# Start of a two-layer decoder trunk: held weight loads, first group's terms by readiness, matmuls over zeros

## What is computed

```python
for l in range(DEPTH):
    y = mixer_sublayer(x, w_in[l], lbs[l], a_norm_w[l], c_sinks[l], w_out[l], cos, sin)
    x = layer_norm(ALPHA * x + y, ln1_g[l], ln1_b[l])
    y = conv_ffn(x, w_gate[l], w_up[l], conv_w[l], conv_b[l], w_down[l])
    x = layer_norm(ALPHA * x + y, ln2_g[l], ln2_b[l])
```

## Time and profile before

| | us |
|---|---|
| median of 3 runs | 2239.49 |
| lowest, highest | 2239.21, 2239.70 |
| the profiled execution, its own time | 2238.69 |
| its span in the profile | 2236.9 |
| TensorE busy | 2207.1 (99%) |
| VectorE busy | 1391.9 (62%) |
| ScalarE busy | 1028.4 (46%) |
| GpSimd busy | 221.6 (10%) |

### The profile page before, as it was taken

How to read it: one execution, slowest core, us unless ns; L and a number is a source line. 1 busy time by engine, 2 the same in 40 slices (tenths; PEclk the granted TensorE clock), 3 DMA queues, 4 the chain that set the end, 5 groups by cost and what they waited for, 6 DMA issues and landing times.

```text
span 2236.9 us, 31431 instructions
## 1 busy us (share of the span) xinstructions
PE 2207.1 (99%) x11372; PEld 1889.1 (84%) x11372; DVE 1391.9 (62%) x1750; ACT 1028.4 (46%) x1286; POOL 221.6 (10%) x245
## 2 busy tenths in 40 slices
PE   8999999999999999999999999999999999999997
PEld 6888887888888888888888888888888888888886
DVE  5556666776666666545485566667766666664545
ACT  5444454544444444333454445554444444443332
POOL 1651000120000000000007310002100000000000
PEclk9999999999999999999999999999999999999999
DMA  8555465666666666666665555656666666666664
GB/s 294 171 163 170 144 221 156 202 189 185 191 188 188 187 188 205 221 194 193 185 193 169 160 160 152 226 164 193 185 191 191 189 182 194 188 226 198 193 193 132
DMA packets 214740, 420.25 MB, mean 188 GB/s; under 512 B 13024, under 2 KB 15104, under 8 KB 213632
## 3 DMA queue, kind: packets, MB, share of 16 engines
q1 hardware_dynamic: 212224, 406.90, 59.9%
q0 software_dynamic: 2432, 12.22, 1.5%
HBM read 416.97 MB, written 2.10 MB: 187 GB/s over the span
## 4 chain that ended last, share of the span: by engine, by line
PE 97%; DVE 1%; POOL 1%; ACT 0%; DMA 0%; issue 0%; DVEq 0%; POOLq 0%; ACTq 0%; SPq 0%
PE ps L1088 29%; PE ps L1044 17%; PE ps L1046 17%; PE ps L1045 17%; PE ps L1092 15%; PE ps L1182 1%; PE ps L1133 1%; PE ps L1156 0%; PE ps L1189 0%; PE ps L1202 0%; PE ps L1203 0%; PE ps L1201 0%; DMA raw<-in_w_in_dram 0%; DVE xres L803 0%; DVE xres L809 0%
## 5 line engine op out<-in xcount | busy, mean ns | idle before, releaser
L734 DVE TENSOR_TENSOR wlo<-raw,whi 128x1024 fp32r<-128x1024 f32 x768 | 952.2, 1246 | 757.2 <-ACT whi L524 753.9
L524 ACT ACTIVATE whi<-raw 128x1024 fp32r<-128x1024 f32 x768 | 807.1, 1058 | 966.5 <-PE ps L1046 460.7
L1088 PE MATMUL ps<-xT,whi 128*128 128x512 f32 x2816 | 657.2, 390 | 1.7 <-DVE xT L744 1.0
L1088 PEld LDWEIGHTS ps<-xT,whi 128*128 128x128 f32 x2816 | 522.4, 188 | 107.8 <-ACT qkT L539 2.1
L1044 PE MATMUL ps<-whi,xT 128*128 128x512 f32 x960 | 385.3, 401 | 9.9 <-DVE wlo L734 9.4
L1046 PE MATMUL ps<-whi,xT 128*128 128x512 f32 x960 | 375.2, 391 | 0.0
L1045 PE MATMUL ps<-wlo,xT 128*128 128x512 f32 x960 | 374.6, 390 | 0.0
L1092 PEld LDWEIGHTS ps<-xT,wlo 128*128 128x128 f32 x2816 | 350.0, 192 | 7.2
L1092 PE MATMUL ps<-xT,wlo 128*128 128x256 f32 x2816 | 352.2, 283 | 0.0
L1046 PE MATMUL ps<-whi,hT 128*128 128x512 f32 x704 | 273.9, 389 | 0.0
L1044 PE MATMUL ps<-whi,hT 128*128 128x512 f32 x704 | 273.9, 389 | 0.0
(11 more groups left out here) (158 smaller groups left out, 1070.5 us busy)
## 6 DMA issues: line engine op xcount, KB each, us to landing
raw<-in_w_in_dram SPq DMA_DIRECT2D x176, 512.0 KB, 3.9
raw<-in_w_gate_dram SPq DMA_DIRECT2D x176, 512.0 KB, 4.3
raw<-in_w_up_dram SPq DMA_DIRECT2D x176, 512.0 KB, 4.2
raw<-in_w_down_dram SPq DMA_DIRECT2D x176, 512.0 KB, 4.6
raw<-in_w_out_dram SPq DMA_DIRECT2D x64, 512.0 KB, 4.6
mix<-in_x_t_dram SPq DMA_DIRECT2D x8, 256.0 KB, 6.8
xres<-in_x_dram POOLq DMA_DIRECT2D x4, 512.0 KB, 8.4
lnb<-in_ln_g_dram POOLq DMA_DIRECT2D x2, 1024.0 KB, 7.8
```

The costliest lines, as they stand in the source:

```text
L524: act.activation(whi[:, s, :, :], raw[:, s, :, :], ACT.Copy).then_inc(hi_done, 1)
L734: dve.tensor_tensor(wlo[:, s, :, :], raw[:, s, :, :], whi[:, s, :, :].bitcast(F32), ALU.subtract)\
L1088: ins = pe.matmul(ps[:, bank, :], whi[:, s, kk, cols], xT[:, kt, :, :].rearrange("p a s -> p (a s)"), start=kt == 0, stop=kt == KT - 1)
```

## The change

Three edits, all at the start of layer 0:

- SyncE waits for the landing of weight group 0 before it issues x 1 (and with it weights 1), and for the landing of group 1 before it issues x 2 (and weights 2). All loads from x 3 on have no new wait.
- TensorE runs the first group by a new function, `first_group`. Its 12 matmuls are ordered by term: four of high weights with high x, which wait for `hi_done` and `xhi_done` only; four of low weights, which wait for `lo_done`; four with the low part of x, which wait for `x_ready`. The other groups are as before.
- VectorE first clears one half of `prob`, and TensorE runs three fp32 matmuls of 384 columns over these zeros into bank 7, whose content is overwritten later.

```diff
+                        if layer == 0 and i == 0 and 1 <= j <= 2:
+                            sp.wait_ge(raw_in[j - 1], 16)
                         if layer == 0 and i == 0:
                             sp.dma_start(mix[:, GK * j:GK * (j + 1), :], x_t[j * GK * P:(j + 1) * GK * P, :].rearrange(
...
+            dve.memset(prob[:, 0, :], 0.0).then_inc(warm_set, 1)
...
+            pe.wait_ge(warm_set, 1)
+            for n in range(3):
+                pe.matmul(ps[:, 7, 0:3 * P], prob[:, 0, 0:P], prob[:, 0, :], start=True, stop=True)
...
+            def first_group():
+
+                pe.wait_ge(hi_done, 1)
+                pe.wait_ge(xhi_done, 1)
+                terms = ((whi, 0), (wlo, 0), (whi, 1))
+                for n, (w, part) in enumerate(terms):
+                    if n == 1:
+                        pe.wait_ge(lo_done, 1 + CREDIT)
+                    if n == 2:
+                        pe.wait_ge(x_ready, 1)
+                    for t, kk in itertools.product(range(TT), range(GK)):
+                        ins = pe.matmul(ps[:, in_banks(0)[t], :], xT[:, kk, part, t * P:(t + 1) * P], w[:, 0, kk, :],
+                                        start=n == 0 and kk == 0, stop=False)
+                ins.then_inc(pe_used, 1)
...
-                        if i == 0:
+                        if i == 0 and layer + j > 0:
                             pe.wait_ge(x_ready, layer * 24 + (j + 1))
...
-                    rows_times_chunk(layer, p, xT, kts, banks, j == 0, j == GC - 1)
+                    if layer + p == 0:
+                        first_group()
+                    else:
+                        rows_times_chunk(layer, p, xT, kts, banks, j == 0, j == GC - 1)
```

More of the change, by code:

```diff
@@ L276, in program @@
         ln1_in, ln2_in = sem("ln1_in"), sem("ln2_in")
-        spare_set = sem("spare_set")
+        spare_set, warm_set = sem("spare_set"), sem("warm_set")
         lb_max, lb_exp = sem("lb_max"), sem("lb_exp")
```

## The result

The changed kernel takes 2244.15 us (median of 16 runs, 2242.22 to 2246.22), the kernel before 2239.32 (16 runs, 2238.33 to 2240.09). The ratio is 1.0021 with a 95% interval of 1.0014 to 1.0028, so the change costs 4.8 us. The spread of the runs more than doubled. The profiled execution of the changed kernel took 2242.95, 1.2 us under its median, and its span is 2241.2 against 2236.9.

The account below looks back on a forecast made before the run. TensorE's string of matmuls, 97% of the last chain, was taken to bound the kernel. Held loads start group 2 at 19.5 against 16.68 us, so 2239.5 + 2.8 = 2242.3 us, range 2239.0 to 2244.6.

Parts of the forecast that it names:

- First group by readiness: TensorE, group 0: first four matmuls wait for high parts alone, landing + 1.2 us instead of + 2.46, so 1.3 us earlier.
- The bound in the text: TensorE's opening wait: zeros even four times as dear would end by 9.2 us, and only then would they push group 0.
- group 0 would run at the low clock: TensorE, group 0: taken at 1.2 GHz, matmuls 0.43 us apart, ending at 12.3 us; said not to enter the sum.
- w0: Weight load of group 0: 4.3 us from issue with nothing behind it, landing at 5.9 us, 1.0 us earlier than before.
- w1 and w2: Weight loads of groups 1 and 2, held back: landing at 10.8 us (9.34 before) and 17.1 us (11.44 before).
- The burst: GpSimd's bias, level, flip, anorm and sinks loads, 0.66 MB, move forward 2 to 4 us and delay group 2's weights 0.4 us.
- w3 and the next land 2.1 us apart: Weight loads behind group 2's land faster than TensorE's 2.7 us per group, so nothing else stops TensorE in this stretch.
- what would prove me wrong: Signs against the forecast, among them TensorE idle ahead of group 3 or later, read as the burst hitting group 3's weights.
- The sum: TensorE: group 1 waits to 13.3 us, group 2 to 19.5 against 16.68, 2.8 us later, with nothing given back behind.
- The rival of the clock: TensorE's 3.5 us gap ahead of group 2 drops the clock, 1.81 us more: 4.6 us later, 2244.1 us, chance 0.16.
- The rival of the gain: All loads at the quick end, group 2's weights before 14.2 us: the hold pays, 2237.8 to 2239.5 us, chance 0.14.
- The rule on DMAs: Issue early, wait late speaks against the two waits; its page's figures give an estimated loss of 1 us.

Follow-up runs that it names:

- no_hold: The changed kernel without SyncE's two waits, zeros and new first group kept: 2237.39 us, ratio 0.9991 to the kernel before.
- hold_only: The kernel before with SyncE's two waits alone, no zeros and first group as before: 2242.29 us, ratio 1.0014.
- first_only: The kernel before with the new first group alone, no zeros and no held loads: 2238.28 us, ratio 0.9997.
- hold_zeros_8: The changed kernel, both waits kept, with eight matmuls over zeros instead of three: 2243.31 us.
- late_burst: The changed kernel with GpSimd's five small loads waiting for group 5 instead of group 0: 2240.48 us, ratio 1.0007 to the kernel before.
- hold_1: The changed kernel with only the first wait (x 1 and weights 1 wait for weights 0): 2239.7 us.
- hold_2: The changed kernel with only the second wait (x 2 and weights 2 wait for weights 1): 2240.05 us.

## Why the prediction was right, and where not

The forecast was 2242.3, slower, by the held loads, with 2239.0 to 2244.6 as the range. 2244.15 lies in it, near its upper end, and the direction and the cause were right: no_hold and hold_only show it. The size was not: 4.8 us slower against the 2.8 forecast.

- **First group by readiness.** Forecast: 1.3 us earlier against the kernel before, plus what the landing gains. The first matmul came 1.35 us earlier, of which 0.2 is the landing. first_only has it at 8.18, 1.2 earlier. Right.
```profile
73.03 1.78 PE ps L1145 x16
```

That makes 0.66 us for 384 columns at the high clock and 4.0 for three at the low one. They ended 1.7 us before the first high part was ready, so they cost nothing. The bound in the text was set against the wrong moment: zeros that end at 9.2 would not have pushed the old start at 9.39, but they would have pushed the new one at 7.1, as eight of them did in hold_zeros_8. That group 0 would run at the low clock was so in the profile for its first half (1.84 us for four matmuls; its last four start at 11.38 and take some 1.1).
- **w0.** Forecast 5.9, measured 6.73. The step "With x0 in front of it but nothing behind, I put w0 at 4.3 us" failed: 5.05 us from issue to landing with nothing behind, against 5.3 in company. Over all profiles it is 4.75 to 5.05 with x 1 held and 4.86 to 5.38 without. The gain that the holds should buy was 0.2 us and not 1.0.
- **w1 and w2.** Forecast 10.8 and 17.1, measured 11.14 and 15.53. From issue to landing both took 4.0 us. w1 came 0.3 us late, w0's 0.8 less what its own load was quicker. For w2 I took 5.3 us because loads would stand behind it, and this term was too large by 1.3. With the 0.4 for the burst, which hit nothing there, w2 came 1.6 us earlier than I said, and group 2 at 17.99 and not at 19.5.
- **The burst.** This is the step that failed most. I gave it 0.4 us, on w2. It hit w4, which took 9.9 us from issue (13.60) to landing (23.53), and cost 3.7 us by late_burst. The step from "w3 and the next land 2.1 us apart" to "nothing else stops TensorE in this stretch" was wrong, since it left out the burst behind w2 while the groups had nothing left in hand. I had named this as what would prove me wrong: idle ahead of group 3 or later. There I had named w3 as what it would hit, but w3 was as late in late_burst, without the burst. The trace of the kernel before had it in plain sight, a landing of 3.3 us instead of 2.1, which was hidden there by 4 us in hand.
- **The sum.** 1.5 us too much for w2 and some 2.5 too little for w4 in the profile, so the two errors offset each other in part, which is luck: group 4 came 3.9 us late against the 2.8 forecast. Of the 4.8 us between the medians the two profiles show 4.2 or 4.3.
- **The rival of the clock.** Its chance was 0.16. It doesn't show in the changed kernel's profile (0.23 us apart behind each gap), and it shows in hold_1's and hold_2's, with gaps of 2.28 and 2.21 us, shorter than I had asked for. The changed kernel's other runs reach 2246.2, and a falling clock would fit them; this is argued, not shown.
- **The rival of the gain.** It wanted w2 before 14.2. With a weight load at 4.0 us and w0 at 6.7 it was out of reach.
- **The rule on DMAs** in the Trainium skill's "DMA: Bandwidth & Descriptors", Rules for kernel authors (issue early, wait late), holds here: each hold alone costs 2.3 to 2.7 us. By the Trainium skill's figures there a 512 KB load is an estimated 3.2 us, and 4.0 were measured. The x load stands just ahead of it: for both, 768 KB, the same figures give an estimated 3.8 us, and 4.4 were measured from the issue of x (6.72 to 11.14, 11.13 to 15.53). The prediction gave w2 near 15 and a loss of 1 us by these figures; measured were 15.53 and group 2 1.3 us late. That is nearer than the 17.1 and 2.8 that I worked out from the rows. What the burst did to group 4, which is most of the loss, is in neither.

## What to carry to other kernels

Holding back a load to hasten the one in front is worth only what that one loses to company, and here this was 0.2 us: compare its time alone and in company before trading a full round trip for it. Each group's time in hand at the start is one common stock. Add up everything that draws on it, the bursts of other queues too, and ask where a burst lands once the stock is used up. Work that only fills a wait can steady the clock, but it shortens the kernel only where nothing else is waited for right behind, and it must end before the real work is ready.

## What the runs showed of the hardware that I had not expected

- The first weight load takes 4.75 to 5.05 us from issue to landing even with nothing behind it, and the same size takes 4.0 a few us later. In the changed kernel, where it lands at 6.73, the engines move 105 GB/s in 5 to 6 us and 18 in 6 to 7, so at the end it doesn't wait for bandwidth. What it waits for isn't shown.
- 0.6 MB from GpSimd's queue took two thirds of the engines' time in 18 to 22 us of the changed kernel, and the total rate in 19 to 22 us was 250 GB/s, where late_burst has 379. The delay to one weight load was 3.1 us, more than the bytes account for (an estimated 1.6 us, 0.6 MB at 374 GB/s). It differs from trace to trace: the same burst cost one landing 1.2 us in the kernel before (3.3 instead of 2.1).
- TensorE's clock was at its low level again behind a gap of 2.28 us in hold_1, after a group at the high one, and fell within a us behind a gap of 2.21 us in hold_2, while gaps of 1.1 to 2.1 us in the changed kernel left it high.
- Each fp32 matmul of 384 columns shows as two rows (x6 for three) and takes about 1.3 us at the low clock (4.18 us for three, with the tail of the last). At the high clock an fp32 matmul of 128 columns took 0.22 us and an fp32 transpose of 128 columns 0.11.
